# GpSimd forms the rests of the output weights in both feed-forwards, and the first feed-forward's gate and up products are laid side by side

## The chip, the cores and the metric

The kernel runs on one core of a Trainium2 chip. The metric is the device time of one execution in microseconds (us). The kernel before took 1524.12 us, the median of 3 runs (1520.59 to 1524.94).

## The reference, cut to what matters

Two transformer blocks follow one another on 256 tokens of width 1024, in float32. The first has attention, a short convolution and a mixture of 32 experts. The second wraps two attentions between two feed-forwards, and those two are what the change touches:

```python
def swiglu(h, w_in, w_out):
    gu = h @ w_in                      # 1024 x (2 * 2816)
    g, u = jnp.split(gu, 2, axis=-1)
    return (jax.nn.silu(g) * u) @ w_out   # 2816 x 1024

ada = c_act @ w_ada[l] + b_ada[l]      # 1024 x 9216, one row
h = modulate(rmsnorm(x, ffn1_norm[l]), sh1, sc1)
x = x + FFN_RES_WEIGHT * g1[:, None, :] * swiglu(h, ffn1_w_in[l], ffn1_w_out[l])
...                                    # two attentions
h = modulate(rmsnorm(x, ffn2_norm[l]), sh3, sc3)
x = x + FFN_RES_WEIGHT * g3[:, None, :] * swiglu(h, ffn2_w_in[l], ffn2_w_out[l])
```

## The kernel before, in words

The five engines run their own instruction lists side by side and meet only at semaphores. Activations lie transposed: the 1024 channels in 8 chunks of 128 partitions, the 256 tokens along the free axis.

**Hi and lo parts.** Each float32 operand of the feed-forwards is split in two: a rounded part ("hi", type fp32r, written by a ScalarE copy) and a rest ("lo", the original less the rounded part). A product is the sum of three: hi weights by hi inputs, lo weights by hi inputs, hi weights by lo inputs. The inputs' parts lie beside each other in `ff_x_parts` (per chunk, 256 columns of hi, then 256 of lo).

**Steps.** The inner width 2816 is cut into 22 steps of 128, s = 1 to 22, for each of the feed-forwards "ffn1" and "ffn2". `past(key)` adds 22 to the semaphore counts of ffn2. Step s has on TensorE a `gate_up` (gate and up, 8 chunks each, three passes) and a `down` (8 output chunks, three passes over the hi and lo parts of weights and activations). TensorE runs `gate_up(s + 1)` between `gate_up(s)` and `down(s)`. Steps 3 to 22 lie in a loop of 5 iterations with four steps written out (j = 0 to 3); `down(22)` is `down_by_bank`, after the loop. The gate and up sums of a step take two PSUM banks, 4 and 5 or 6 and 7 by the step's parity.

**ffn1 against ffn2.** They differ in `gate_up`. In ffn1 it is 48 matmuls of 256 columns (L1680, L1690, L1698), all summed into the first half of the banks. In ffn2, from the second step on, the hi weights meet hi and lo inputs in one matmul of 512 columns (L1685, 16 of them), which leaves the product with the lo inputs in the second half of the bank; then come the 16 matmuls with the lo weights (L1690). ScalarE copies the second halves out to `ff_b` (L1045), VectorE adds both halves into `gate_up_sum` (`sum_halves`, L2410), and ScalarE applies Silu there (L1049). In ffn1 Silu reads the bank itself (L1040) and VectorE takes "up" from the bank.

**VectorE's list** per step: the rest of the output weights (`ff_out_rest`, L2376, 128x1024, both inputs in SBUF), `sum_halves` (ffn2 only), silu(gate) times up (`act`, L2418), the rest of the next step's input weights (`ff_rest`, L2369, 128x2048), and the rest of the activation (`act_rest`, L2423).

**The ada columns.** ffn1 carries other work along: 10 pieces of `c_act @ w_ada` of 512 columns each, two in an iteration. VectorE sums a piece over 8 chunks in 8 dependent instructions (`mod_steps`, L2434 for the first, L2437 for the other seven) into `mod_acc`; of the 16 instructions of an iteration 5 stand at the end of VectorE's step j=0, 5 at the end of j=1 and 6 at the end of j=2. TensorE folds each piece over the partitions (`ada_columns`, L1740) after the `gate_up` of its j=1 (first piece) and of its j=2 (second), and waits there for the last instruction of the piece:

```python
pe.wait_ge(sem("mod_acc_step"), it * 16 + 8 * (u + 2))
pe.wait_ge(sem("ff_act"), s)
```

TensorE's j=1 `gate_up` is that of step 4it+4, its j=2 one that of 4it+5; VectorE's j counts from s = 4it+2. VectorE's `take_columns` (L2445) adds the bias to the folded piece, in j=2 and j=3.

**Queues.** ScalarE's list per step: round half of a new input weight chunk (`ff_round`, L1026), silu, round a new half of the output weights (`ff_round_out`, L1032; the half of step s comes behind the silu of step s-1), round the activation (L1054). SP issues all weight loads of this stage. GpSimd has nothing from the convolution (L762 to L766) until the first feed-forward's end, then a few small masks (L772 to L786), and one DMA in the second feed-forward (L789). Nothing is planned at run time; the order of each list is written out by hand.

Of the kernel before, what the change touches and what calls it, by code (L numbers as in the profile page):

```python
# [14 lines left out]
T = 256  # L15
# [137 lines left out]
def mixed_blocks_kernel(nc, ins, out):  # L153
# [3 lines left out]
    with ExitStack() as ctx:  # L157
# [577 lines left out]
        def _(pool):  # L735
# [31 lines left out]

            pool.wait_ge(sem("bias_stored"), 16)
# [14 lines left out]
            for at in (64, P + 192):  # L783
                late = ca_bias[64:P, :, at:at + 64]
                step(nc.gpsimd.tensor_scalar(late, late, NEG, 1.0, ALU.add, ALU.mult))
            nc.gpsimd.memset(pool_done[:, :], 0.0).then_inc(sem("masked"), 1)  # L786
            pool.wait_ge(sem("ff_x_lo"), 2 * KD)
            g_at = ROWS_B["final_norm"]
            pool.dma_start(gain_rows, ins["vectors_b"][g_at:g_at + KD, :].rearrange("r c -> (r c)").partition_broadcast(P))\  # L789
                .then_inc(sem("gain_rows_loaded"), 16)  # L790

# [5 lines left out]
        def _(act):  # L797
# [237 lines left out]
            def feed_forward(key):  # L1035
                def silu(s, parity, more=True):

                    act.wait_ge(sem("ff_gate_up_done"), s + past(key))
                    if key == "ffn1":
                        nc.scalar.activation(gate_up_sum[:, parity, 0, :], bank[4 + 2 * parity][:, 0:T], ACT.Silu)\  # L1040
                          .then_inc(sem("ff_silu"), 1)
                        return
                    if more:
                        act.wait_ge(sem("ff_summed"), s - 1)
                    nc.scalar.activation(ff_b[:, :, :], psum[:, 4 + 2 * parity:6 + 2 * parity, T:2 * T], ACT.Copy)\  # L1045
                      .then_inc(sem("ff_b_taken"), 1)
                    act.wait_ge(sem("ff_summed"), s)
                    gate = gate_up_sum[:, parity, 0, :]
                    nc.scalar.activation(gate, gate, ACT.Silu).then_inc(sem("ff_silu"), 1)  # L1049

                def round_act(s, parity):

                    act.wait_ge(sem("ff_act"), s + past(key))
                    nc.scalar.activation(ff_act_hi[:, parity, :], gate_up_sum[:, parity, 1, :], ACT.Copy)\  # L1054
                      .then_inc(sem("ff_act_hi"), 1)

                ff_round_out(key, 3, 0, 16)
                silu(1, 0, more=False)
                round_act(1, 0)
                ff_round_out(key, 3, 1, 16)  # L1060
                with act.Fori(0, FF_LOOPS) as it:
                    for j in range(4):
                        slot = 2 * (j // 2)
                        ff_round(key, slot, j % 2, it * 32 + 32 * (1 + j // 2))
                        silu(it * 4 + j + 2, (j + 1) % 2)
                        ff_round_out(key, slot + 1, j % 2, it * 16 + 16 * (1 + j // 2))
                        round_act(it * 4 + j + 2, (j + 1) % 2)
                silu(4 * FF_LOOPS + 2, 1)
                round_act(4 * FF_LOOPS + 2, 1)

# [112 lines left out]
        def _(pe):  # L1183
# [479 lines left out]
            def feed_forward(key, ada_items):  # L1663
                all_emptied(JOBS[done_jobs[0] - 1])

                def gate_up(s, slot, half, parity, taken, first=False):
# [4 lines left out]
                    if taken is not None and key == "ffn1":  # L1671
                        pe.wait_ge(sem("ff_act"), taken)
                    elif taken is not None:
                        pe.wait_ge(sem("ff_summed"), taken)
                    if first or key == "ffn1":
# [12 lines left out]
                    for g in range(2):  # L1688
                        for k in range(KD):
                            last = pe.matmul(to[g][:, 0:T], lhsT=w_lo[:, k, g, :], rhs=ff_x_hi[:, k, :], start=False,  # L1690
                                             stop=(k == KD - 1 and key == "ffn2"), skip_group_check=True)
                    if first or key == "ffn1":
                        at = 0 if key == "ffn1" else T
                        for g in range(2):
                            for k in range(KD):
                                if g == 0 and first:
                                    pe.wait_ge(sem("ff_x_lo"), k + 1 + past(key, KD))
                                last = pe.matmul(to[g][:, at:at + T], lhsT=w_hi[:, k, g, :], rhs=ff_x_lo[:, k, :], start=False,  # L1698
                                                 stop=(k == KD - 1), skip_group_check=True)
# [201 lines left out]
        def _(dve):  # L1901
# [470 lines left out]
            def ff_out_rest(key, s, slot, half):  # L2372

                dve.wait_ge(sem("ff_out_hi"), s + past(key))
                part = slice(half * D, (half + 1) * D)
                nc.vector.tensor_tensor(ff_out_lo[slot][:, part], ring(slot)[:, part], ff_out_hi[slot][:, part], ALU.subtract)\  # L2376
                  .then_inc(sem("ff_out_lo"), 1)

# [25 lines left out]
            def feed_forward(key, with_ada, gate_at):  # L2404
                def sum_halves(s, parity):

                    if key == "ffn1":
                        return
                    dve.wait_ge(sem("ff_b_taken"), s)
# [3 lines left out]
                def act(s, parity):  # L2413
# [3 lines left out]
                    by = bank[5 + 2 * parity][:, 0:T] if key == "ffn1" else up  # L2417
                    nc.vector.tensor_tensor(up, gate_up_sum[:, parity, 0, :], by, ALU.mult).then_inc(sem("ff_act"), 1)  # L2418
# [29 lines left out]
                ff_out_rest(key, 1, 3, 0)  # L2448
# [6 lines left out]
                with dve.Fori(0, FF_LOOPS) as it:  # L2455
                    for j in range(4):
                        s, parity = it * 4 + j + 2, (j + 1) % 2
                        ff_out_rest(key, s, (3, 1, 1, 3)[j], (j + 1) % 2)
# [8 lines left out]
                ff_out_rest(key, 4 * FF_LOOPS + 2, 3, 1)  # L2467
# [242 lines left out]
```

## Time and profile before

| what | us |
|---|---|
| median of 3 runs | 1524.12 (1520.59 to 1524.94) |
| the profiled execution | 1516.13 |
| its span, first to last instruction | 1514.1 |
| TensorE busy in it | 1459.4 (96%) |
| VectorE busy | 617.6 (41%) |
| ScalarE busy | 443.2 (29%) |
| GpSimd busy | 27.3 (2%) |
| ffn1, first to last matmul of gate, up and down | 903.3 to 1102.8 |
| ffn2, the same | 1317.2 to 1504.2 |

The profiled execution took 2.0 us more than its span, and it is 8.0 us shorter than the median of the runs. An engine's share of busy time is a mean over stages with different limits. Times in the rows below are counted from the span's start.

### The profile page before, as it was taken

The page shows a single profiled execution, that of the slowest core. Times are in us where ns is not written, and L with a number is a line of the kernel's source. Part 1 is how long each engine was busy: PE and PEld are TensorE (multiplying, and loading weights), DVE is VectorE, ACT ScalarE, POOL GpSimd, SP SyncE. Part 2 cuts the span into 40 slices and gives each one's busy share as a digit, 9 for nine tenths or more (in the row PEclk, how much of TensorE's full clock was granted, in tenths as well). Part 3 has the DMA queues.
Part 4 walks back from the last instruction along what each step waited for, and adds up shares of the span by engine and source line. Part 5 has one row for each costly group of instructions (what it writes and reads, how often), then busy time and mean ns, then how long its engine had stood idle before and what let it go on. Part 6 is the DMA issues. An engine that isn't in the chain of part 4 may idle for free.

```text
span 1514.1 us, 23559 instructions
## 1 busy us (share of the span) xinstructions
PE 1459.4 (96%) x9994; PEld 1029.7 (68%) x9994; DVE 617.6 (41%) x1024; ACT 443.2 (29%) x674; POOL 27.3 (2%) x36
## 2 busy tenths in 40 slices
PE   6999999999999999999999999999999998999997
PEld 3986854444444444444434459999999777999997
DVE  5686240011110001101100038777777577565555
ACT  3434031111011111111011134333354364454443
POOL 0011000000000000000000000000020000000000
PEclk9999999999999999999999989999999999999999
DMA  9959799999999999999999997888667731355651
GB/s 357 354 189 351 286 385 431 425 429 431 425 431 427 431 424 430 427 429 430 429 429 427 427 340 245 283 286 295 230 220 276 258 112 53 120 171 181 207 172 56
DMA packets 117427, 481.01 MB, mean 318 GB/s; under 512 B 12108, under 2 KB 59465, under 8 KB 96769
## 3 DMA queue, kind: packets, MB, share of 16 engines
q1 hardware_dynamic: 115936, 476.46, 80.4%
q0 software_dynamic: 736, 2.31, 0.5%
q10 hardware_dynamic: 705, 1.51, 0.3%
q8 instruction: 39, 0.64, 0.2%
q14 instruction: 11, 0.09, 0.0%
HBM read 479.20 MB, written 1.06 MB: 317 GB/s over the span
## 4 chain that ended last, share of the span: by engine, by line
PE 73%; DMA 21%; DVE 3%; ACT 2%; issue 1%; SPq 0%; DVEq 0%; ACTq 0%
DMA arena<-in_w_up_dram 18%; PE psum L1576 14%; PE psum L1712 8%; PE psum L1790 7%; PE psum L1598 6%; PE psum L1690 6%; PE psum L1685 5%; PE psum L1215 3%; PE psum L1680 3%; PE psum L1698 3%; PE psum L1339 3%; PE psum L1557 2%; PE psum L1539 2%; DMA arena<-in_w_mod_dram 2%; DMA arena<-in_ffn_w_in_dram 1%
## 5 line engine op out<-in xcount | busy, mean ns | idle before, releaser
L1576 PE MATMUL psum<-arena,squares 128*64 128x384 f32 x2048 | 339.3, 489 | 21.0 <-DMA arena<-in_w_up_dram 12.3
L1576 PEld LDWEIGHTS psum<-arena,squares 128*64 128x64 f32 x2048 | 146.3, 137 | 216.3 <-issue 186.0
L2303 DVE TENSOR_TENSOR mixT<-mixT,psum 128x384 f32<-128x384 f32 x32 | 26.5, 827 | 496.7 <-PE psum L1576 496.7
L1598 PE MATMUL psum<-arena,small 128*64 128x512 f32 x768 | 171.9, 596 | 0.0
L1598 PEld LDWEIGHTS psum<-arena,small 128*64 128x64 f32 x768 | 52.3, 137 | 96.2 <-issue 94.4
L2369 DVE TENSOR_TENSOR ff_w_lo<-arena,ff_w_hi 128x2048 fp32r<-128x2048 f32 x44 | 100.6, 2285 | 0.0
L1690 PE MATMUL psum<-ff_x_parts,ff_w_lo 128*128 128x256 f32 x704 | 91.5, 283 | 0.0
L1690 PEld LDWEIGHTS psum<-ff_x_parts,ff_w_lo 128*128 128x128 f32 x704 | 88.9, 192 | 1.6
L1026 ACT ACTIVATE ff_w_hi<-arena 128x2048 fp32r<-128x2048 f32 x44 | 84.0, 1908 | 0.2 <-DMA arena<-in_ffn_w_in_dram 0.2
L1685 PE MATMUL psum<-ff_x_parts,ff_w_hi 128*128 128x512 f32 x336 | 79.7, 389 | 0.0
L998 ACT ACTIVATE small<-psum 128x384 f32<-128x384 f32 x32 | 15.8, 493 | 212.5 <-PE psum L1584 212.5
L1790 PE MATMUL psum<-ff_x_parts,mid_w_hi 128*128 128x256 f32 (+1 forms) x576 | 75.9, 287 | 0.1
L1557 PE MATMUL psum<-small 64*128 64x256 f32 x528 | 74.6, 402 | 0.7 <-ACT small L1003 0.7
L1790 PEld LDWEIGHTS psum<-ff_x_parts,mid_w_hi 128*128 128x128 f32 (+1 forms) x576 | 71.1, 190 | 2.9 <-ACT ff_x_parts L880 1.4
L1003 ACT ACTIVATE small<-psum 128x512 f32<-128x512 f32 x32 | 19.1, 598 | 176.6 <-PE psum L1598 176.6
L1685 PEld LDWEIGHTS psum<-ff_x_parts,ff_w_hi 128*128 128x128 f32 x336 | 61.7, 188 | 11.6
L1079 ACT ACTIVATE mid_w_hi<-arena 128x2048 fp32r<-128x2048 f32 (+2 forms) x28 | 45.8, 1644 | 73.1 <-PE psum L1790 56.4
L1557 PEld LDWEIGHTS psum<-small 64*128 64x128 f32 x528 | 45.5, 186 | 29.0 <-issue 24.5
L1539 PE MATMUL psum<-mixT,h_rows 128*128 128x128 f32 x512 | 59.8, 275 | 0.0
L2383 DVE TENSOR_TENSOR mid_w_lo<-arena,mid_w_hi 128x2048 fp32r<-128x2048 f32 (+2 forms) x28 | 54.7, 1955 | 12.4 <-ACT mid_w_hi L1079 12.3
L1539 PEld LDWEIGHTS psum<-mixT,h_rows 128*128 128x128 f32 x512 | 58.5, 192 | 0.1
L996 ACT ACTIVATE mixT<-psum 128x384 f32<-128x384 f32 x32 | 15.7, 491 | 140.4 <-PE psum L1576 140.4
(344 smaller groups left out, 1966.9 us busy)
## 6 DMA issues: line engine op xcount, KB each, us to landing
arena<-in_w_gate_dram SPq DMA_DIRECT2D x32, 3072.0 KB, 32.8
arena<-in_w_up_dram SPq DMA_DIRECT2D x31, 3072.0 KB, 33.9
arena<-in_w_down_dram SPq DMA_DIRECT2D x31, 3072.0 KB, 32.2
arena<-in_ffn_w_in_dram SPq DMA_DIRECT2D x44, 1024.0 KB, 7.6
arena<-in_w_ada_dram SPq DMA_DIRECT2D x18, 2048.0 KB, 12.6
arena<-in_w_mod_dram SPq DMA_DIRECT2D x11, 2048.0 KB, 14.0
arena<-in_ffn_w_out_dram SPq DMA_DIRECT2D x22, 1024.0 KB, 4.9
arena<-in_w_in_dram SPq DMA_DIRECT2D x10, 2048.0 KB, 9.8
```

The costliest lines, as they stand in the source:

```text
L1026: nc.scalar.activation(ff_half(ff_w_hi[slot], half), ff_half(ring(slot), half), ACT.Copy)\
L1079: nc.scalar.activation(hi, raw, ACT.Copy).then_inc(sem("mid_hi"), 1)
L1539: last = pe.matmul(b[:, k * P:(k + 1) * P], lhsT=h_rows[:, tb, (4 * part + k) * P:(4 * part + k + 1) * P], rhs=pick[:, tb, :], start=(tb = ...
L1557: last = pe.matmul(bank[m // 2][:, (m % 2) * T:(m % 2 + 1) * T], lhsT=y_e[64 * half:64 * half + 64, c * P:(c + 1) * P], rhs=pick_wT[64 * h ...
L1576: last = pe.matmul(b[64 * half:64 * half + 64, 0:HALF_E], lhsT=xeT[:, k, u * SLOTS:(u + 1) * SLOTS], rhs=w[:, k, half * HALF_E:(half + 1) ...
L1598: last = pe.matmul(bank[6][64 * half:64 * half + 64, :], lhsT=hiddenT[:, f % 3, 64 * (f // 3):64 * (f // 3) + 64], rhs=down[:, f, half * 5 ...
L1685: last = pe.matmul(to[g][:, :], lhsT=w_hi[:, k, g, :], rhs=ff_x_parts[:, k, :, :], start=(k == 0), stop=False, skip_group_check=True)
L1690: last = pe.matmul(to[g][:, 0:T], lhsT=w_lo[:, k, g, :], rhs=ff_x_hi[:, k, :], start=False, stop=(k == KD - 1 and key == "ffn2"), skip_gro ...
L1712: last = pe.matmul(bank[m // 2][:, (m % 2) * T:(m % 2 + 1) * T], lhsT=w[slot][:, half * D + m * P:half * D + (m + 1) * P], rhs=x[:, parity ...
L1790: last = pe.matmul(b[0:n, c * T:(c + 1) * T], lhsT=w[:, k, lo:lo + n], rhs=x[:, k, :], start=opens and c == 0 and k == 0, stop=closes and ...
L2369: nc.vector.tensor_tensor(ff_half(ff_w_lo[slot], half), ff_half(ring(slot), half), ff_half(ff_w_hi[slot], half), ALU.subtract).then_inc(se ...
L2383: nc.vector.tensor_tensor(lo, raw, hi, ALU.subtract).then_inc(sem("mid_lo"), 1)
```

## The change

In four places: `ff_out_rest` goes from VectorE's list to GpSimd's, for both feed-forwards; `silu` and `sum_halves` take the way with `ff_b` in both; `gate_up` uses the 512-column matmuls in ffn1 too, from its second step on; and the waits that used `ff_act` or bare counts in ffn1 now use `ff_summed` with `past(key)`. The ada columns stay where they are.

```diff
 @block.gpsimd
+            def ff_out_rest(key, s, slot, half):
+                pool.wait_ge(sem("ff_out_hi"), s + past(key))
+                part = slice(half * D, (half + 1) * D)
+                nc.gpsimd.tensor_tensor(ff_out_lo[slot][:, part], ring(slot)[:, part], ff_out_hi[slot][:, part], ALU.subtract)\
+                  .then_inc(sem("ff_out_lo"), 1)
+            def feed_forward(key):
+                for it in range(FF_LOOPS):
+                    for j in range(4):
+                        ff_out_rest(key, it * 4 + j + 2, (3, 1, 1, 3)[j], (j + 1) % 2)
+                ff_out_rest(key, 4 * FF_LOOPS + 2, 3, 1)
+            ff_out_rest("ffn1", 1, 3, 0)
+            feed_forward("ffn1")
             pool.wait_ge(sem("bias_stored"), 16)
             pool.wait_ge(sem("ffn1_sum_done"), 4)
...
             nc.gpsimd.memset(pool_done[:, :], 0.0).then_inc(sem("masked"), 1)
+            ff_out_rest("ffn2", 1, 3, 0)
             pool.wait_ge(sem("ff_x_lo"), 2 * KD)
...
+            feed_forward("ffn2")
 @block.scalar, silu
-                    if key == "ffn1":
-                        nc.scalar.activation(gate_up_sum[:, parity, 0, :], bank[4 + 2 * parity][:, 0:T], ACT.Silu)\
-                          .then_inc(sem("ff_silu"), 1)
-                        return
                     if more:
-                        act.wait_ge(sem("ff_summed"), s - 1)
+                        act.wait_ge(sem("ff_summed"), s - 1 + past(key))
 @block.tensor, gate_up
-                    if taken is not None and key == "ffn1":
-                        pe.wait_ge(sem("ff_act"), taken)
-                    elif taken is not None:
-                        pe.wait_ge(sem("ff_summed"), taken)
-                    if first or key == "ffn1":
+                    if taken is not None:
+                        pe.wait_ge(sem("ff_summed"), taken + past(key))
+                    if first:
...
-                    if first or key == "ffn1":
-                        at = 0 if key == "ffn1" else T
+                    if first:
 @block.vector
-            def ff_out_rest(key, s, slot, half):
...
 feed_forward, sum_halves
-                    if key == "ffn1":
-                        return
-                    dve.wait_ge(sem("ff_b_taken"), s)
+                    dve.wait_ge(sem("ff_b_taken"), s + past(key))
 act
-                    by = bank[5 + 2 * parity][:, 0:T] if key == "ffn1" else up
-                    nc.vector.tensor_tensor(up, gate_up_sum[:, parity, 0, :], by, ALU.mult).then_inc(sem("ff_act"), 1)
+                    nc.vector.tensor_tensor(up, gate_up_sum[:, parity, 0, :], up, ALU.mult).then_inc(sem("ff_act"), 1)
```

## Rows read from the trace of the kernel before

**Rows 1.** Busy time by stretch, inside ffn1: window, length, engines, PEclk, DMA share, GB/s.
```profile
960.00:1000.00 40.00, 40.00 (x339) 40.00 (x338) 30.60 (x37) 16.48 (x20) 0.00 (x0) 1.00 0.87 299
```
**Rows 2.** Timeline of ffn1: start, length, engine, line, operation, shapes, count [idle before].
```profile
952.64 1.11 PE L1712 MATMUL psum<-ff_act_hi,ff_out_hi 128*128 128x256 f32 x8
...
961.23 1.11 PE L1712 MATMUL psum<-ff_act_hi,ff_out_hi 128*128 128x256 f32 x8
...
969.82 0.95 PE L1740 MATMUL psum<-consts,mod_acc 128*128 128x1 f32 x8
...
973.88 4.69 DVE L2437 SCALAR_TENSOR_TENSOR mod_acc<-arena,cond,mod_acc 128x512 f32<-128x512 f32 x6
...
979.29 0.94 PE L1740 MATMUL psum<-consts,mod_acc 128*128 128x1 f32 x8
```
**Rows 3.** VectorE by line, 920 to 1080: count | busy us, mean ns | idle before.
```profile
L2437 DVE SCALAR_TENSOR_TENSOR mod_acc<-arena,cond,mod_acc 128x512 f32<-128x512 f32 x64 | 48.1, 751 | 2.0
...
L2434 DVE TENSOR_SCALAR mod_acc<-arena,cond 128x512 f32<-128x512 f32 x10 | 4.8, 482 | 1.1 <-DMA arena<-in_w_ada_dram 1.1
```
**Rows 4.** Timeline of one step of ffn2.
```profile
1372.45 1.11 PE L1712 MATMUL psum<-ff_act_hi,ff_out_hi 128*128 128x256 f32 x8
...
1373.28 0.69 DVE L2410 TENSOR_TENSOR small<-psum,ff_b 128x512 f32<-128x512 f32 x1 [3.04 <-ACT ff_b L1045]
...
1374.33 1.05 ACT L1032 ACTIVATE ff_out_hi<-arena 128x1024 fp32r<-128x1024 f32 x1
...
1374.46 0.42 DVE L2418 TENSOR_TENSOR small<-small 128x256 f32<-128x256 f32 x1 [0.48 <-ACT small L1049]
1374.80 2.29 DVE L2369 TENSOR_TENSOR ff_w_lo<-arena,ff_w_hi 128x2048 fp32r<-128x2048 f32 x1
...
1375.29 3.79 PE L1685 MATMUL psum<-ff_x_parts,ff_w_hi 128*128 128x512 f32 x16
...
1377.00 0.42 DVE L2423 TENSOR_TENSOR ff_act_lo<-small,ff_act_hi 128x256 fp32r<-128x256 f32 x1
1377.34 1.22 DVE L2376 TENSOR_TENSOR ff_out_lo<-arena,ff_out_hi 128x1024 fp32r<-128x1024 f32 x1
...
1380.84 1.11 PE L1712 MATMUL psum<-ff_act_hi,ff_out_hi 128*128 128x256 f32 x8
```
**Rows 5.** Timelines of GpSimd and VectorE beside each other, in the convolution.
```profile
110.95 2.36 POOL L765 TENSOR_TENSOR arena<-arena,mixT 128x1024 f32<-128x1024 f32 x1
...
115.56 2.61 POOL L765 TENSOR_TENSOR arena<-arena,mixT 128x1024 f32<-128x1024 f32 x1
...
115.46 0.49 DVE L2135 TENSOR_SCALAR small<-small,stats 128x512 f32<-128x512 f32 x1
...
115.86 2.60 DVE L2135 TENSOR_SCALAR small<-small,stats 128x512 f32<-128x512 f32 x1
```
**Rows 6.** The same two engines behind ffn1.
```profile
1110.64 0.70 POOL L780 TENSOR_SCALAR arena<-arena,consts 2x512 f32<-2x512 f32 x1
1111.43 0.75 POOL L781 TENSOR_SCALAR arena<-arena,consts 2x512 f32<-2x512 f32 x1
...
1110.95 0.65 DVE L2389 SCALAR_TENSOR_TENSOR ff_x_parts<-hT,ada,ff_x_parts 128x256 fp32r<-128x256 f32 x1
...
1111.53 0.92 DVE L2389 SCALAR_TENSOR_TENSOR ff_x_parts<-hT,ada,ff_x_parts 128x256 fp32r<-128x256 f32 x1
...
1109.00 0.86 DVE L1975 SCALAR_TENSOR_TENSOR hT<-xT,gains,psum 128x256 f32<-128x256 f32 x2
```
**Rows 7.** Timeline, VectorE at the start of ffn1.
```profile
912.76 3.25 DVE L1981 SCALAR_TENSOR_TENSOR xT<-xT,cols_a,rstd 128x256 f32<-128x256 f32 x8
```
**Rows 8.** TensorE's pauses in the expert stage: waits (total, times, longest), timeline, stretch.
```profile
PE psum L1576 <- DMA arena<-in_w_up_dram: 12.3, 7, 1.9
...
544.16 12.23 PE L1576 MATMUL psum<-arena,squares 128*64 128x384 f32 x64 [3.38 <-issue]
...
545.00:550.00 5.00, 5.00 (x24) 1.99 (x20) 0.00 (x0) 0.00 (x0) 0.00 (x0) 0.66 1.04 436
```

More of the change, by code:

```diff
@@ L1038, in silu @@
                     act.wait_ge(sem("ff_gate_up_done"), s + past(key))
-                    if key == "ffn1":
-                        nc.scalar.activation(gate_up_sum[:, parity, 0, :], bank[4 + 2 * parity][:, 0:T], ACT.Silu)\
-                          .then_inc(sem("ff_silu"), 1)
-                        return
                     if more:
-                        act.wait_ge(sem("ff_summed"), s - 1)
+                        act.wait_ge(sem("ff_summed"), s - 1 + past(key))
                     nc.scalar.activation(ff_b[:, :, :], psum[:, 4 + 2 * parity:6 + 2 * parity, T:2 * T], ACT.Copy)\
                       .then_inc(sem("ff_b_taken"), 1)
-                    act.wait_ge(sem("ff_summed"), s)
+                    act.wait_ge(sem("ff_summed"), s + past(key))
                     gate = gate_up_sum[:, parity, 0, :]
@@ L1690, in gate_up @@
                             last = pe.matmul(to[g][:, 0:T], lhsT=w_lo[:, k, g, :], rhs=ff_x_hi[:, k, :], start=False,
-                                             stop=(k == KD - 1 and key == "ffn2"), skip_group_check=True)
-                    if first or key == "ffn1":
-                        at = 0 if key == "ffn1" else T
+                                             stop=(k == KD - 1), skip_group_check=True)
+                    if first:
                         for g in range(2):
                             for k in range(KD):
-                                if g == 0 and first:
+                                if g == 0:
                                     pe.wait_ge(sem("ff_x_lo"), k + 1 + past(key, KD))
-                                last = pe.matmul(to[g][:, at:at + T], lhsT=w_hi[:, k, g, :], rhs=ff_x_lo[:, k, :], start=False,
+                                last = pe.matmul(to[g][:, T:2 * T], lhsT=w_hi[:, k, g, :], rhs=ff_x_lo[:, k, :], start=False,
                                                  stop=(k == KD - 1), skip_group_check=True)
@@ L2370, in ff_rest @@
                                         ALU.subtract).then_inc(sem("ff_w_lo"), 1)
-            def ff_out_rest(key, s, slot, half):
[L2374 to L2377, printed above, removed]
             def rest_w(name):
@@ L2446, in take_columns @@
                                             ALU.add).then_inc(sem("ada_col_read"), 1)
-                ff_out_rest(key, 1, 3, 0)
                 sum_halves(1, 0)
@@ L2466, in feed_forward @@
                             mod_steps(it, 5 * j, 5 * j + 5 + j // 2)
-                ff_out_rest(key, 4 * FF_LOOPS + 2, 3, 1)
                 sum_halves(4 * FF_LOOPS + 2, 1)
```

1 line of the change is left out of this document (removed).

## The prediction

> **What bounds the kernel now.** I read the busy times by stretch first. In 40 us of ffn1 TensorE is busy for all 40.00 at full clock, VectorE for 30.60, GpSimd for none [rows 1]. So ffn1 is bound by TensorE, and VectorE, at three quarters, is the engine to watch. The timeline gives TensorE's pace as the distance between two downs: 961.23 - 952.64 = 8.59 us for a plain step. With ada columns in it a step takes 979.29 - 969.82 = 9.47 us [rows 2]. An iteration of the loop is 2 x 8.59 + 2 x 9.47 = 36.12 us. The same timeline shows where VectorE comes close: the six `mod_steps` of j=2 start at 973.88 and end at 978.57, and TensorE takes their result at 979.29 [rows 2]. That slack of 0.72 us is the smallest in the loop. In ffn2 a step takes 1380.84 - 1372.45 = 8.39 us [rows 4].
>
> **The change, part by part.** Sums are against the profiled execution (1516.13 us). It ran 8.0 us under the median of the runs; I carry the difference over to the median.
>
> *Fewer, wider matmuls.* ffn2 already has the form that ffn1 gets, and its plain step is 8.59 - 8.39 = 0.20 us shorter [rows 2, 4]. Steps 2 to 22 get it: 21 x 0.20 = 4.2 us, if nothing else binds. A step with ada columns would take 9.27.
>
> *A longer chain behind a gate_up.* From the end of `gate_up` (G = 1372.45, where the down starts) rows 4 give VectorE's times: sum at G+0.83, `act` at G+2.01, `ff_rest` at G+2.35, `act_rest` at G+4.55, next operation at G+4.89. ScalarE ends the new rounded output half at G+2.93. The sum adds 0.69 us of work to VectorE in ffn1, the move takes off 1.22 [rows 4]; by work alone VectorE has 0.5 us less per step.
>
> *GpSimd's subtraction.* 44 of 128x1024. Its own tensor_tensor of that size took 2.36 and 2.61 us [rows 5], against VectorE's 1.22 [rows 4]. GpSimd is idle here [rows 1], and the rest of step s may be ready as late as down(s), a whole step after its rounded half, so its length alone costs nothing. But the two engines hold each other up. In rows 5 a VectorE tensor_scalar started at 115.46 took 0.49; GpSimd's subtraction-sized operation, issued at 115.56, took 0.25 longer than the other one and ended at 118.17; and the next VectorE operation, the same as the first, took 2.60, to 118.46. Taken apart: GpSimd ended 2.22 after VectorE's first (115.95), was served before an instruction already queued, and VectorE resumed 0.20 before GpSimd's end (118.46 - 0.49 = 117.97). Is it so for operations with two SBUF inputs, such as those of ffn1? Rows 6 say yes: two of L2389 beside two short GpSimd operations took 0.65 and 0.92, while eight of that size with two SBUF inputs took 3.25 without GpSimd, 0.41 each [rows 7]; the second GpSimd operation took 0.05 more than the first. An operation with one input in PSUM (L1975, 0.86 for two) ran on undisturbed [rows 6]. So `sum_halves` is free of it; `act`, `ff_rest`, `act_rest` and the `mod_steps` are not.
>
> By the Trainium skill (SBUF — State Buffer, Who interferes with whom) a VectorE instruction with two SBUF inputs and a GpSimd instruction that reads SBUF exclude each other for the whole instruction. By that rule the sum is the one below; rows 5 and 6 agree, with blocks of 2.1 us and 0.2 to 0.5 us.
>
> *What it does to a step.* GpSimd may start at G+2.93, but `ff_rest` has run since G+2.35 and ends at G+4.64. GpSimd then ends at 4.64 + 2.22 = 6.86, and `act_rest` starts at 6.66 in place of 4.55: 2.11 us lost. In ffn2 VectorE would still be done at G+7.1, before the next sum at 8.39 + 0.83 = 9.22, and the third pass of the down that needs `act_rest` comes later still. So ffn2 keeps its time: 0. The ends of this cost are 0 and 0.5 us for its start; I take 0. The DMA of the gains, now queued on GpSimd behind the first rest, is used only at the end.
>
> *What it does to ffn1.* The `mod_steps` stand behind it. They take 0.75 each with 0.48 for the first of a piece [rows 3]: 3.5 us at j=0, 3.5 at j=1, 4.69 to the end of the six at j=2 [rows 2]. A VectorE step is now 1.18 (sum to act) + 0.34 + 2.20 + 2.11 + 0.34 = 6.17 us before its mod steps. From j=0 on, 6.17 + 3.5 = 9.7 is more than the 8.39 of TensorE, so VectorE falls behind and the chain runs through it. With G of j=0 at 0:
> - j=0's sum starts at 0.83; the three steps take 3 x 6.17 + 3.5 + 3.5 + 4.69 = 30.2, so the second piece is ready at 31.0.
> - TensorE waits for the first piece until 0.83 + 2 x 6.17 + 3.5 + 2.25 = 18.9, where it came at 2 x 8.39 = 16.8: a stall of 2.1 us. It is back at 18.9 + 9.27 = 28.2, and waits 2.8 us for the second.
> - From there ada columns, down and gate_up take 9.27; the next G of j=0 is at 40.3. VectorE has no mod steps at j=3 and has caught up by then.
>
> Per iteration 40.3 - 36.1 = 4.2 us more, and 5 x 4.2 = 21.0. The saving of the wide matmuls is inside that.
>
> *Start and end.* VectorE runs eight operations with two SBUF inputs (3.25 us) behind step 1 [rows 7], and GpSimd's second rest falls into them. They end 2.1 us later, sum(2) with them, at about 2.2 us past the 0.83 that the chain above starts from: 2.2 more, once. Step 2's own saving is 0.2. At the end of ffn1 the down of step 21 covers 2.84 us (1375.29 - 1372.45), while `act` starts at 2.01 [rows 4] and has itself and ScalarE's rounding, 0.4 each, before `down_by_bank`: 0.2 more than before. Together 21.0 + 2.2 - 0.2 + 0.2 = 23.2.
>
> *The clock.* The stalls of 2.1 and 2.8 us are new. Pauses up to 1.9 us in the expert stage (7 of them) go with full clock; after one of 3.38 us the granted clock was 0.66 over 5 us [rows 8], part of that at the lower level (1.2 GHz), which costs 0.34 x 5 = 1.7 us. 2.8 lies between. A loss behind the first piece is swallowed by the wait for the second; behind the second it counts, five times: 0 to 8.5. I take the middle, 4.3, since the nearest rows on both sides are about equally far.
>
> *Other queues.* SP loads the next ada chunk when the first piece is summed, 2 us later than now; what is queued behind it waits for a down that is later anyway. ScalarE's silu waits for `sum_halves` and so is late with VectorE, and with it the next rounding of input weights; these are wanted a down and more later. 0.
>
> Sum: 23.2 + 4.3 = 27.5. The profiled execution would be 1543.6, the median 1524.12 + 27.5 = 1551.6 us.
>
> **The rivals.**
>
> *GpSimd does not hold VectorE up in ffn1* (not slower). For it: rows 5 are of a one-input operation, and rows 6 of short ones; neither is two tensor_tensors. Against it: rows 6 show the same order of service. Then j=2's mod steps end at G + 4.89 + 4.69 = 9.58 against TensorE's 9.27, a wait of 0.3 to 0.4 us, where 0.8 is saved in an iteration: 5 x 0.43 = 2.2 faster, with start and end still 2.2: 1521.9. It decides from the point at which VectorE loses under about 0.5 us a step.
>
> *GpSimd holds VectorE up by part.* In rows 6 VectorE lost (0.65 - 0.47) + (0.92 - 0.47), 0.63 us, beside 1.45 us of GpSimd's work: 0.43 for one. (0.47 is one such operation from issue to end, 0.41 the pace.) At that rate, or if GpSimd is let in only in VectorE's gaps, a subtraction costs 1.0: the step is 5.06, the second piece is ready at 0.83 + 15.2 + 11.7 = 27.7, the iteration is 37.0, 5 x 0.9 = 4.5 more, 1.0 at the start; TensorE's stall is 1.6 and the clock stays. 1529.6.
>
> *The full block without the clock's part* is 1547.3; *with all of it*, 1555.8; these are the ends of the likeliest case, with 4 us around them for the lengths of the blocks.
>
> **How the numbers follow.** Full block 0.76 (1543 to 1560); block by part 0.10; no block 0.10; anything else, such as TensorE's wide matmuls not saving their 0.2, 0.04. The range, 1529 to 1563, takes in the partial block and leaves out the last two. A difference under 0.3% (4.6 us) can't be told from none. The no-block case, at 2.2 us, is inside that: faster 0.04, same 0.11, slower 0.85.
>
> **What would show it.** In the changed kernel's profile: L1685's form in ffn1 with 227 ns or so from one to the next; GpSimd busy for some 100 us more, with operations of 2.4 to 4 us from issue to end; VectorE's `act_rest` or the operation behind `ff_rest` about 2.1 us longer in ffn1 and ffn2, `sum_halves` still 0.69; TensorE's idle time before L1740, released by VectorE's L2437, of about 2 us and 2.8 us in each iteration; ffn2 as long as before; PEclk under 1.00 in some stretches of ffn1. I am wrong if `act_rest` keeps its 0.42 and there is no wait before L1740.

## The result, and the profile after

The changed kernel took 1548.0 us, the median of 4 runs (1545.6 to 1554.2), against 1522.4 (1519.6 to 1524.9) for the kernel before on the same chip: 1.0183 times as long [1.0159, 1.0206]. That is 25.6 us more by the medians and 28 by the ratio. 1551.6 was forecast, 27.5 more. The profiled execution took 1545.67 us, with a span of 1543.5.

The page of the changed kernel: the span; busy time by engine; the granted clock; two of the costliest groups (instruction and line, shapes, count | busy us, mean ns of one | idle before it).

```profile
span 1543.5 us, 22902 instructions
...
PE 1467.5 (95%) x9648; PEld 1022.5 (66%) x9658; DVE 670.9 (43%) x1002; ACT 455.4 (30%) x696; POOL 193.8 (13%) x80
...
PEclk9999999999999999999999999999999999899999
...
L772 POOL TENSOR_TENSOR ff_out_lo<-arena,ff_out_hi 128x1024 fp32r<-128x1024 f32 x44 | 166.7, 3790 | 1212.9 <-ACT ff_out_hi L1051 1212.9
...
L2425 DVE TENSOR_TENSOR ff_act_lo<-small,ff_act_hi 128x256 fp32r<-128x256 f32 x44 | 106.5, 2420 | 1.9 <-ACT ff_act_hi L1069 1.9
```

VectorE gave 44 subtractions of 1.22 us away (53.7 us) and took 22 sums of 0.69 (15.1 us), and yet is busy for 53.3 us more than the 617.6 before. `act_rest` (L2425), which took 0.42 us before [rows 4], takes 2.42 in the mean over its 44: 2.62 in 40 of them, and 0.42 or so in the four that have no `ff_rest` before them. A digit of PEclk stands for 39 us, and its 9 for anything from 0.9 up: too coarse to show what the clock did in ffn1. Shorter stretches show it, in experiment 7.

TensorE's waits in ffn1, between 900 and 1130 us: what waited for what, total us, times, longest us. In the kernel before VectorE's last mod step was 0.72 us ahead [rows 2].

```profile
PE psum L1752 <- DVE mod_acc L2439: 18.5, 10, 2.6
PE psum L1703 <- DVE ff_w_lo L2381: 1.4, 2, 1.2
```

The ada columns wait all ten times. The timeline of the second iteration, some of its lines on TensorE, VectorE and GpSimd, with the idle time before a line and its releaser in brackets, answers to [rows 2]:

```profile
960.21 1.11 PE L1724 MATMUL psum<-ff_act_hi,ff_out_hi 128*128 128x256 f32 x8
...
961.12 0.69 DVE L2413 TENSOR_TENSOR small<-psum,ff_b 128x512 f32<-128x512 f32 x1 [5.42 <-ACT ff_b L1060]
...
962.64 2.28 DVE L2381 TENSOR_TENSOR ff_w_lo<-arena,ff_w_hi 128x2048 fp32r<-128x2048 f32 x1
...
963.29 3.88 POOL L772 TENSOR_TENSOR ff_out_lo<-arena,ff_out_hi 128x1024 fp32r<-128x1024 f32 x1 [7.87 <-ACT ff_out_hi L1051]
964.84 2.62 DVE L2425 TENSOR_TENSOR ff_act_lo<-small,ff_act_hi 128x256 fp32r<-128x256 f32 x1
967.38 0.47 DVE L2436 TENSOR_SCALAR mod_acc<-arena,cond 128x512 f32<-128x512 f32 x1
...
970.92 0.68 DVE L2413 TENSOR_TENSOR small<-psum,ff_b 128x512 f32<-128x512 f32 x1
...
979.55 1.05 PE L1752 MATMUL psum<-consts,mod_acc 128*128 128x1 f32 x8 [2.41 <-DVE mod_acc L2439]
...
986.85 4.68 DVE L2439 SCALAR_TENSOR_TENSOR mod_acc<-arena,cond,mod_acc 128x512 f32<-128x512 f32 x6
...
991.59 1.05 PE L1752 MATMUL psum<-consts,mod_acc 128*128 128x1 f32 x8 [2.48 <-DVE mod_acc L2439]
...
992.50 2.02 PE L1724 MATMUL psum<-ff_act_hi,ff_out_hi 128*128 128x256 f32 x8
...
1002.52 0.76 PE L1724 MATMUL psum<-ff_act_hi,ff_out_hi 128*128 128x256 f32 x5
```

The lines to see are the fourth and fifth. GpSimd is released at 963.29, while `ff_rest` runs on VectorE until 964.92. It ends at 967.17, 2.25 us behind that; `act_rest`, issued next on VectorE, lasts until 967.46, 2.62 us where 0.42 would do: 2.20 late. The mod steps come behind it, and then the next `sum_halves`, which has no idle time before it any more: VectorE sets the pace.

**Where the time went.** I count iterations from down to down: the first starts with the down behind `gate_up(2)`, which runs while VectorE does its j=0 (in what follows, a "down of j=0"). It starts at 915.78, and the one behind the fifth iteration at 1124.81: 209.03 us, against 5 x 36.12 = 180.60 before: 28.4 us more. The iterations last 44.43, 42.31, 40.77, 40.76 and 40.76. That is 40.77 for the chain, 5 x 4.65 = 23.2 in all; a later start of 2.1; and 1.55 in each of the first two, in which the clock had fallen behind the second wait. Outside the loop the two profiled executions differ by 1.0 us in all: 0.7 less before it and 1.7 more behind it.

ffn2, the timeline of one of its steps; it answers to [rows 4]:

```profile
1385.12 1.11 PE L1724 MATMUL psum<-ff_act_hi,ff_out_hi 128*128 128x256 f32 x8
...
1387.47 2.29 DVE L2381 TENSOR_TENSOR ff_w_lo<-arena,ff_w_hi 128x2048 fp32r<-128x2048 f32 x1
...
1388.12 3.88 POOL L772 TENSOR_TENSOR ff_out_lo<-arena,ff_out_hi 128x1024 fp32r<-128x1024 f32 x1 [4.50 <-ACT ff_out_hi L1051]
1389.67 2.62 DVE L2425 TENSOR_TENSOR ff_act_lo<-small,ff_act_hi 128x256 fp32r<-128x256 f32 x1
...
1393.50 0.76 PE L1724 MATMUL psum<-ff_act_hi,ff_out_hi 128*128 128x256 f32 x5
```

The same hold-up of 2.20 us, and a step of 8.38, as before: nothing waits for VectorE here. From the first down of ffn2 to its last bank it is 172.97 us in both kernels (1330.52 to 1503.49 before, 1359.96 to 1532.93 now).

### The profile page after: what moved, and what is told of

Same layout as the page of the kernel before. It is cut to its first block, busy times and chain, and to the rows that moved or that the text cites. A ratio compares the mean times of both kernels' runs of the same rounds, so it can differ in the third digit from the quotient of the medians.

```text
span 1543.5 us, 22902 instructions
## 1 busy us (share of the span) xinstructions
PE 1467.5 (95%) x9648; PEld 1022.5 (66%) x9658; DVE 670.9 (43%) x1002; ACT 455.4 (30%) x696; POOL 193.8 (13%) x80
## 4 chain that ended last, share of the span: by engine, by line
PE 62%; DMA 20%; DVE 11%; issue 3%; ACT 3%; SPq 0%; DVEq 0%; ACTq 0%
DMA arena<-in_w_up_dram 17%; PE psum L1591 14%; PE psum L1802 7%; PE psum L1698 6%; PE psum L1613 6%; PE psum L1724 5%; PE psum L1703 3%; PE psum L1230 3%; DVE mod_acc L2439 3%; PE psum L1354 3%; DVE ff_act_lo L2425 3%; PE psum L1572 2%; PE psum L1554 2%; DMA arena<-in_w_in_dram 2%; DMA arena<-in_ffn_w_in_dram 1%
## 5 line engine op out<-in xcount | busy, mean ns | idle before, releaser
L772 POOL TENSOR_TENSOR ff_out_lo<-arena,ff_out_hi 128x1024 fp32r<-128x1024 f32 x44 | 166.7, 3790 | 1212.9 <-ACT ff_out_hi L1051 1212.9
L1698 PE MATMUL psum<-ff_x_parts,ff_w_hi 128*128 128x512 f32 x672 | 159.9, 390 | 0.0
L1698 PEld LDWEIGHTS psum<-ff_x_parts,ff_w_hi 128*128 128x128 f32 x672 | 123.7, 188 | 23.4
L2425 DVE TENSOR_TENSOR ff_act_lo<-small,ff_act_hi 128x256 fp32r<-128x256 f32 x44 | 106.5, 2420 | 1.9 <-ACT ff_act_hi L1069 1.9
L1060 ACT ACTIVATE ff_b<-psum 128x512 f32<-128x512 f32 x44 | 26.4, 599 | 161.3 <-PE psum L1703 159.6
```

Of the source, the lines that this page charges most:

```text
L772: nc.gpsimd.tensor_tensor(ff_out_lo[slot][:, part], ring(slot)[:, part], ff_out_hi[slot][:, part], ALU.subtract)\
L1698: last = pe.matmul(to[g][:, :], lhsT=w_hi[:, k, g, :], rhs=ff_x_parts[:, k, :, :], start=(k == 0), stop=False, skip_group_check=True)
L2425: nc.vector.tensor_tensor(ff_act_lo[:, parity, :], gate_up_sum[:, parity, 1, :], ff_act_hi[:, parity, :], ALU.subtract).then_inc(sem("ff_a ...
```

## The experiments

Ratios are to the kernel before, run on the same chip, whose medians were 1521.5 to 1522.0 us. Profiled executions of nearly equal programs differ by up to 8 us in when ffn1 starts (its first down of j=0 at 915.8 to 924.2). They differ so before anything in which the kernels do: the sums of squares for ffn1's norm start on TensorE at 891.8 in the kernel before and at 900.0 in experiment 1; so within ffn1 I compare lengths of iterations, from a down to the down four steps later, and not spans.

**1. Rests back on VectorE.** The changed kernel without its GpSimd part: what do the wide matmuls and the sum cost alone?

```diff
 @block.gpsimd
-            ff_out_rest("ffn1", 1, 3, 0)
-            feed_forward("ffn1")
...
-            ff_out_rest("ffn2", 1, 3, 0)
...
-            feed_forward("ffn2")
 @block.vector, where it stands in the kernel before
+                nc.vector.tensor_tensor(ff_out_lo[slot][:, part], ring(slot)[:, part], ff_out_hi[slot][:, part], ALU.subtract)
```

> The changed kernel with both feed-forwards' output-weight rests back on VectorE; ffn1 keeps the 512-column matmuls and the summing of halves. Theory (GpSimd blocks VectorE, VectorE's mod steps hold TensorE up): no operation behind ff_rest is stretched, so act_rest is 0.42 us again. Per iteration VectorE's sum is late by 0.3 and 0.6 us at j=1 and j=2, the second piece is 1.0 us late, and the iteration takes 36.3 us against 36.1 before and 40.8 to 44.4 in the changed kernel: 1 us over the kernel before in all, the whole 25 us of the change gone. Rival (the longer chain of copy, sum and Silu in ffn1 costs the time, GpSimd little): 15 us or more stay. Rival (the wide matmuls do not save): iterations of 37 us and more, some 5 us over the kernel before.

Measured: 1526.3 us, 1.0026 [1.0011, 1.0042], 4 us over before by the ratio (4.8 by the medians), and some 22 under the changed kernel. TensorE's waits in its ffn1:

```profile
PE psum L1748 <- DVE mod_acc L2442: 5.0, 6, 1.4
```

Its timeline, TensorE in the first iteration and a later one:

```profile
953.07 2.05 PE L1720 MATMUL psum<-ff_act_hi,ff_out_hi 128*128 128x256 f32 x8
963.05 1.11 PE L1720 MATMUL psum<-ff_act_hi,ff_out_hi 128*128 128x256 f32 x8
...
1026.50 1.05 PE L1748 MATMUL psum<-consts,mod_acc 128*128 128x1 f32 x8 [0.83 <-DVE mod_acc L2442]
...
1035.89 1.11 PE L1720 MATMUL psum<-ff_act_hi,ff_out_hi 128*128 128x256 f32 x8
```

The steady iteration is 36.42 us (999.47 to 1035.89), 0.30 more than before. The first is 39.03 (from 924.02), 2.61 longer: a wait of 1.42 before the second piece, and behind it a step of 9.98 where the steady ones take 8.47, with a granted clock of 0.66 from 953 to 958. 5 x 0.30 + 2.61 = 4.1. I had expected 1 us and had left the clock out.

**2. The move alone.** The kernel before, with the GpSimd part of the change: narrow matmuls, no sum in ffn1.

```diff
-                ff_out_rest(...)      # in VectorE's list
+            feed_forward("ffn1")      # in GpSimd's, with ff_out_rest as in the change
```

> The kernel before with only the move: both feed-forwards' rests on GpSimd, ffn1 with its narrow matmuls and no summing of halves. Theory: act_rest grows to 2.6 us here too. VectorE's step before its mod steps is 0.34 + 2.20 + 2.2 + 0.34 = 5.1 us, against 6.2 in the changed kernel, where the wait for copy and sum is added; from G+0.62 three steps and 11.7 us of mod steps give the second piece at 27.5 where TensorE comes at 26.7: an iteration of 37.1 us, 5 us over five iterations and 1 at the start, 6 us over the kernel before. So the two parts do not add up: 6 here, 1 for the other part alone, 25 together. Rival (GpSimd's block costs the same wherever it is): 20 us or more over the kernel before. Rival (no cost without the summing): within 1 us of the kernel before.

Measured: 1536.7 us, 1.0088 [1.0059, 1.0118], 13 us over before, about twice what I expected. TensorE's waits in its ffn1, then GpSimd and VectorE at one step j=3:

```profile
PE psum L1759 <- DVE mod_acc L2449: 6.9, 5, 1.4
```
```profile
1031.22 2.38 POOL L772 TENSOR_TENSOR ff_out_lo<-arena,ff_out_hi 128x1024 fp32r<-128x1024 f32 x1 [5.00 <-ACT ff_out_hi L1051]
...
1032.78 2.96 DVE L2388 TENSOR_TENSOR ff_w_lo<-arena,ff_w_hi 128x2048 fp32r<-128x2048 f32 x1
```

The steady iteration is 37.77 us (1002.97, 1040.74, 1078.52, 1116.28), 1.65 over before: 5 x 1.65 = 8.3. I had expected 37.1; the sum had left out that VectorE stands still for 0.47 us before `take_columns` in j=2. The first iteration is 3.2 longer than the steady ones: 1.5 of it is the clock (955.00 to 965.20, 10.20 us, against 8.67), and 1.65 lie in its first step, with a wait of 1.4 for `ff_w_lo`. In j=3 the order is the other way round: GpSimd comes first, and `ff_rest` is held up for 0.68 us (2.96 in place of 2.28) while `act_rest` keeps its 0.41. The same happened in that first step, where `ff_rest` took 4.16. So the engine that is already at work goes on, and the other waits.

The parts do not add up. The loop of ffn1 is 4.1 us longer with the one, 11.4 with the other and 28.4 with both; a steady iteration +0.30, +1.65 and +4.65. The slack of 0.72 us [rows 2], which each alone may use, is only a small part of that. The rest is how many hold-ups are paid for. In the move alone VectorE's j=0 with its mod steps lasts 8.63 us (1003.59 to 1012.22), close to TensorE's 8.59, so that only the second piece is waited for, five times in all. In the changed kernel it lasts 9.80 (961.12 to 970.92) against 8.39: VectorE falls behind in every step, and both pieces are waited for.

**3. GpSimd in ffn2 only.** The changed kernel, with `ff_out_rest` on VectorE where the key is "ffn1" and on GpSimd where it is "ffn2".

```diff
 @block.gpsimd
-            ff_out_rest("ffn1", 1, 3, 0)
-            feed_forward("ffn1")
 @block.vector
+                if key == "ffn1":
+                    ff_out_rest(key, ...)
```

> The changed kernel with ffn1's rests on VectorE and only ffn2's on GpSimd. Theory: in ffn2 there are no mod steps, VectorE is done at G+7.2 with the block in it and the next sum comes at G+9.2; act_rest takes 2.6 us in ffn2 and 0.42 in ffn1, ffn2's step stays 8.39, and the time is that of e1_vector_rests (4 us over the kernel before) within 2. Rival (GpSimd's work in ffn2 costs too): 8 us or more over the kernel before.

Measured: 1531.3 us, 1.0049 [1.0030, 1.0069]. That is 3.5 us over experiment 1 by the ratios and 5.0 by the medians, with intervals that overlap, where I expected less than 2. VectorE between 1360 and 1500 us, by line:

```profile
L2430 DVE TENSOR_TENSOR ff_act_lo<-small,ff_act_hi 128x256 fp32r<-128x256 f32 x17 | 44.5, 2618 | 0.0
```

And its timeline, two of TensorE's downs in ffn2:

```profile
1388.70 1.11 PE L1722 MATMUL psum<-ff_act_hi,ff_out_hi 128*128 128x256 f32 x8
1397.09 1.11 PE L1722 MATMUL psum<-ff_act_hi,ff_out_hi 128*128 128x256 f32 x8
```

VectorE is held up (in experiment 1 the same instruction takes 0.42 there) and the step is 8.39 us with and without it (1388.16 to 1396.55 in experiment 1). From the first down of ffn2 to its last bank both take 172.97 us (1346.77 to 1519.74 here, 1346.23 to 1519.20 there). The loop of ffn1 is 3.2 us longer than experiment 1's (187.91 against 184.71), though both are the same program there: two more steps at a low clock (1025.04 to 1035.06, 1063.02 to 1073.05: 10.02 us each against 8.47). The two profiled executions as wholes differ by 0.7 us. So ffn2's part costs nothing that shows; that the difference between the medians comes from the clock in ffn1 is likely, but not shown.

**4. GpSimd only writes.** In place of the subtraction GpSimd sets the rest to zero, which reads nothing; the rests of the output weights are left out.

```diff
-                nc.gpsimd.tensor_tensor(ff_out_lo[slot][:, part], ring(slot)[:, part], ff_out_hi[slot][:, part], ALU.subtract)\
+                nc.gpsimd.memset(ff_out_lo[slot][:, part].bitcast(F32), 0.0)\
```

> The changed kernel with GpSimd's subtraction replaced by a memset of the same 128x1024: the rest of the output weights is left out. It writes SBUF and reads nothing, and should take 0.9 us. Theory (VectorE and GpSimd exclude each other where both read SBUF): act_rest 0.42 us, VectorE never delayed by GpSimd, a wait of 0.4 us before the second piece's ada columns, 2 us under the kernel before to 2 over it (the clock may fall after the small waits). Rival (any GpSimd operation on these tiles holds VectorE up): act_rest 0.42 + 0.7 us and more, as in the run with one input.

Measured: 1520.7 us, 0.9995 [0.9976, 1.0014]. GpSimd and VectorE in its ffn1, by line:

```profile
L772 POOL MEMSET ff_out_lo<- 128x1024 f32 x16 | 15.3, 956 | 127.8 <-ACT ff_out_hi L1051 127.8
...
L2425 DVE TENSOR_TENSOR ff_act_lo<-small,ff_act_hi 128x256 fp32r<-128x256 f32 x16 | 6.7, 418 | 0.0
```

TensorE's waits there:

```profile
PE psum L1752 <- DVE mod_acc L2439: 1.0, 5, 0.2
```

`act_rest` is back at 0.42 us. The memset runs beside `ff_rest`, which keeps its 2.29 us (1031.05 to 1032.01 beside 1030.42 to 1032.71), where the subtraction ended 2.25 behind it. The iteration is 35.78 in the mean of five, with one wait of 0.19 in it. This is the first rival's case built: for it I had worked out 36.12 - 0.43 = 35.69, a wait of 0.3 to 0.4 and 2.2 us under before; the ratio says 0.8 under, between 3.7 under and 2.1 over.

**5. GpSimd reads one input.** Between the two: a one-input operation of the same size; the rests hold zeros and so are left out again.

```diff
+                nc.gpsimd.tensor_scalar(ff_out_lo[slot][:, part], ring(slot)[:, part], 0.0, 0.0, ALU.mult, ALU.add)\
```

> The changed kernel with GpSimd's subtraction replaced by a tensor_scalar of the raw weights, 128x1024, one SBUF input: the rest is left out (zeros take its place). About 1.1 us of its own, close to the memset. Theory: it reads SBUF, so it waits for ff_rest to end and act_rest is 0.8 to 0.9 us late (1.3 us from issue to end); VectorE's step is 4.9 us before its mod steps, the second piece is 0.9 to 1.3 us late at TensorE, and the time is 2 to 8 us over the kernel before, between the memset and the changed kernel. Rival (only two-input operations of GpSimd block): act_rest 0.42 and the time of the memset.

Measured: 1531.9 us, 1.0058 [1.0036, 1.0081], 9 us over before. The same two lines:

```profile
L772 POOL TENSOR_SCALAR ff_out_lo<-arena 128x1024 fp32r<-128x1024 f32 x15 | 39.0, 2601 | 102.7 <-ACT ff_out_hi L1051 102.7
...
L2425 DVE TENSOR_TENSOR ff_act_lo<-small,ff_act_hi 128x256 fp32r<-128x256 f32 x15 | 19.0, 1265 | 0.0
```

TensorE's waits:

```profile
PE psum L1752 <- DVE mod_acc L2439: 6.0, 6, 1.1
```

`act_rest` is 1.27 - 0.42 = 0.85 us late, and the iteration is 36.70 at full clock, in the second and the fifth. In the other three the clock fell for a step (38.97, 38.24 and 38.27 us). So of the 8.3 us that its loop is longer than before, the five iterations make 5 x 0.58 = 2.9, the clock some 4.6 and the start 0.8. Experiments 4, 5 and the changed kernel make a scale in which only GpSimd's operation differs: VectorE held up by 0, 0.85 and 2.20 us a step, iterations of 35.78, 36.70 and 40.77. With 0.85 a step of VectorE and its mod steps last 6.17 - 2.11 + 0.85 + 3.5 = 8.41 us, as long as TensorE's 8.39: the first two steps keep up, and one 0.85 is paid for, at the second piece (0.92 an iteration). From there every step adds up: 1.35 more costs 4.07, about three times 1.35.

By the Trainium skill (SBUF — State Buffer, Who interferes with whom) a VectorE instruction with two inputs in SBUF is kept out by a GpSimd instruction that reads SBUF, not by one that only writes. The three runs agree: 0 us beside the memset, 0.85 and 2.20 beside the readers.

**6. Short mod steps.** The changed kernel, GpSimd's subtraction in place, with each mod step on 64 columns of 512; seven eighths of the ada products are left out.

```diff
-                          mod_acc[:, u, :]  ...  w[:, j, :]
+                          mod_acc[:, u, 0:64]  ...  w[:, j, 0:64]
```

> The changed kernel with its rests on GpSimd; the mod steps of ffn1 work on 64 of the 512 columns, so 7 in 8 of the ada columns' products are left out. Theory: the block is as before (act_rest 2.6 us), but 16 mod steps take 3 us and not 11.5, VectorE's step with them is under 8.39 us, TensorE waits for nothing and an iteration takes 35.3 us: 4 us under the kernel before in ffn1, at most 1 lost at its start. Rival (TensorE, ScalarE or the DMAs are slowed by GpSimd's work directly): 10 us or more over the kernel before.

Measured: 1522.1 us, 0.9990 [0.9970, 1.0010], where I expected some 3 us fewer; the interval reaches to 4.6 fewer. GpSimd and VectorE by line:

```profile
L772 POOL TENSOR_TENSOR ff_out_lo<-arena,ff_out_hi 128x1024 fp32r<-128x1024 f32 x16 | 62.2, 3888 | 79.1 <-ACT ff_out_hi L1051 79.1
L2425 DVE TENSOR_TENSOR ff_act_lo<-small,ff_act_hi 128x256 fp32r<-128x256 f32 x16 | 41.9, 2621 | 0.0
```

Its timeline, TensorE's downs of j=0:

```profile
995.72 1.11 PE L1724 MATMUL psum<-ff_act_hi,ff_out_hi 128*128 128x256 f32 x8
...
1031.04 1.11 PE L1724 MATMUL psum<-ff_act_hi,ff_out_hi 128*128 128x256 f32 x8
...
1066.36 1.11 PE L1724 MATMUL psum<-ff_act_hi,ff_out_hi 128*128 128x256 f32 x8
```

`act_rest` is still 2.20 us late and now costs nothing: the iteration is 35.32 us, as long as in experiment 9 without the hold-up, 0.80 under before. Only the first is longer, by 1.30, from the late start. The loop is 2.7 us shorter than before (177.90 against 180.60), which the medians don't show. The hold-up alone is harmless; it costs because the mod steps stand behind it and a wait of TensorE behind them.

**7. Filling the waits.** The changed kernel, with matmuls of zeros before each wait for the mod steps, so that TensorE doesn't pause.

```diff
+                    pe.wait_ge(sem("ff_act"), s)
+                    keep_busy(9, 4 + 2 * u)
                     pe.wait_ge(sem("mod_acc_step"), it * 16 + 8 * (u + 2))
-                    pe.wait_ge(sem("ff_act"), s)
```

> The changed kernel, with matmuls of zeros (9, 4 + 2u of about 0.24 us, some 2 us) put before each wait of TensorE for VectorE's mod steps, so that the wait holds no long pause. They take the time of the wait and nothing else, unless a wait was shorter than they are. My theory: of the 25.6 us over the kernel before, some 3 are lost to the clock that fell behind the wait for the second piece of the ada columns (two of five iterations, 1.55 us each), the rest is the chain on VectorE. Then the granted clock is 1.00 behind those waits, iterations 2 to 5 last 40.8 us each, and the time is about 3 us below the changed kernel: 1.016 of the kernel before. Rival A, the clock costs nothing of the total, since the chain sets the pace: 1.018. Rival B, the clock is the main cost and the iterations return towards 37 us: below 1.008.

Measured: 1544.7 us, 1.0159 [1.0121, 1.0197]. The medians put it 3 us below the changed kernel, and the interval holds both 1.016 and 1.018; the traces decide. A stretch of ffn1: window, length, busy us (instructions) of TensorE, its weight loads, VectorE, ScalarE and GpSimd, granted clock, DMA share, GB/s. With the zeros:

```profile
960.00:1000.00 40.00, 39.03 (x254) 33.77 (x253) 34.44 (x34) 16.26 (x20) 15.81 (x4) 1.00 0.75 262
```

The same stretch of the changed kernel:

```profile
960.00:1000.00 40.00, 35.12 (x226) 32.28 (x225) 34.42 (x34) 16.31 (x20) 15.81 (x4) 0.96 0.72 246
```

With the zeros the clock is 1.00, in the three stretches of 40 us that follow too, and the iterations last 42.88, 40.77, 40.77, 40.76 and 40.77: 205.95 us, 3.08 less than the changed kernel's 209.03. So the clock's part is 3.1 us, and the other 25.3 of the loop's 28.4 are VectorE's chain with its late start.

**8. The second piece a step later.** Can the wait be moved away? The changed kernel, with the second piece folded at TensorE's j=3 in place of j=2, and the 16 mod steps spread 5, 3, 4, 4 over VectorE's four steps in place of 5, 5, 6, 0. `take_columns` for that piece goes to the end of VectorE's j=3, and both pieces are folded in bank 4.

```diff
 @block.tensor, gate_up and down of j=2, then of j=3
-                                ada_columns(it, 1, s - 1)
...
+                                ada_columns(it, 1, s - 1)
 @block.vector
-                            mod_steps(it, 5 * j, 5 * j + 5 + j // 2)
+                            mod_steps(it, (0, 5, 8, 12)[j], (5, 8, 12, 16)[j])
```

> The changed kernel with its rests still on GpSimd, but the second ada piece folded by TensorE after the gate_up of its j=3 and no longer of its j=2, and VectorE's 16 mod steps spread 5, 3, 4, 4 over all four steps. Theory: the block stays (act_rest 2.6 us), but VectorE's idle time at j=3 is used: its iteration is 4 x 6.26 + 11.5 = 36.6 us and it is bound by VectorE's own total, 0.6 us over the kernel before; with the start 3 to 6 us over the kernel before, 20 less than the changed kernel, stalls before the ada columns under 0.5 us. Rival (the time goes by the block itself, wherever the mod steps are waited for): within 5 us of the changed kernel.

Measured: 1553.2 us, 1.0199 [1.0176, 1.0223]; I expected 3 to 6 us over before, and it is 31. TensorE's waits in its ffn1:

```profile
PE psum L1752 <- DVE mod_acc L2439: 14.8, 10, 2.6
```

Its timeline, TensorE in the second iteration and the start of the third:

```profile
980.44 1.05 PE L1752 MATMUL psum<-consts,mod_acc 128*128 128x1 f32 x8 [0.92 <-DVE mod_acc L2439]
981.35 1.39 PE L1724 MATMUL psum<-ff_act_hi,ff_out_hi 128*128 128x256 f32 x8
...
991.36 1.11 PE L1724 MATMUL psum<-ff_act_hi,ff_out_hi 128*128 128x256 f32 x8
...
1001.61 1.05 PE L1752 MATMUL psum<-consts,mod_acc 128*128 128x1 f32 x8 [1.71 <-DVE mod_acc L2439]
1002.52 1.95 PE L1724 MATMUL psum<-ff_act_hi,ff_out_hi 128*128 128x256 f32 x8
```

My error was to add up work over the iteration only. Each piece ends in mod steps that VectorE does in the very step in which TensorE wants them. From the sum at G+0.83 to the end of `act_rest` are 6.26 us, and the four mod steps before the second piece are 3.1 more: ready at G+10.2, wanted at G+8.4. So there is a wait before every piece however light the rest of the iteration is. Besides, nearly every step behind one lasts 10.0 us in place of 8.47 (981.35 to 991.36 and 1002.52 to 1012.52), also behind the wait of 0.92.

**9. Its repair.** The same places for the ada columns, the rests on VectorE, and each rest formed at the end of the step before, behind the mod steps.

```diff
+                        ff_out_rest(key, s + 1, (1, 1, 3, 3)[j], j % 2)   # VectorE, last in its step
```

> The same places of the ada work as in e5_ada_late, with the rests on VectorE (each formed at the end of the step before). A candidate to beat the kernel before. Theory: nothing holds TensorE up in ffn1, iterations of 2 x 8.39 + 2 x 9.27 = 35.3 us, 5 x 0.8 = 4 us under the kernel before, no idle time of TensorE before the ada columns. Rival (the wide matmuls save nothing, or the ada columns still wait): the same as before or above it.

Measured: 1520.4 us, 0.9985 [0.9969, 1.0001]: 28 us faster than the changed kernel, and from the kernel before it can't be told apart. TensorE's waits in its ffn1:

```profile
...
PE psum L1748 <- DVE mod_acc L2442: 0.2, 1, 0.2
```

Its timeline, TensorE at one piece and at two downs four steps apart:

```profile
987.55 0.95 PE L1748 MATMUL psum<-consts,mod_acc 128*128 128x1 f32 x8
...
996.83 1.11 PE L1720 MATMUL psum<-ff_act_hi,ff_out_hi 128*128 128x256 f32 x8
...
1032.15 1.11 PE L1720 MATMUL psum<-ff_act_hi,ff_out_hi 128*128 128x256 f32 x8
```

The iteration is 35.32 us, as in experiment 6: the whole 0.80 of the wide matmuls arrives. Of the 5 x 0.8 = 4.0 us the ratio shows 2.3, and its interval reaches from 4.7 under to 0.2 over.

## Why the prediction was right

The time, 1548.0 against 1551.6, the sign and the mechanism came out as predicted. By its steps:

- *Wide matmuls, 0.20 a step.* Right: without waits the iteration is 35.32 (experiments 6 and 9) against 36.12, 0.80 for four steps. In the changed kernel the step without ada columns is 8.39 too (960.21 to 968.60), but the waits swallow what is saved.
- *GpSimd holds VectorE up by 2.11 us a step.* 2.20 measured, in ffn1 and in ffn2. The order was as read from the convolution [rows 5]: GpSimd ended 2.25 behind VectorE's running instruction (2.22 predicted) and was served before `act_rest`. [rows 5] show it for a VectorE operation with one input, so of the two it is [rows 6] that bear on the rule for two inputs, and the changed kernel bears it out. The rival of no hold-up is refuted by the trace of the changed kernel, and experiment 4 shows what it would have been worth. The rival of a hold-up by part, 1.0 us a step, is refuted too. Experiment 5 is near its size, 0.85; that its 1531.9 us are near the 1529.6 put down for this rival is partly luck: 4.6 of the 8.3 us in its trace are the clock, which the rival had at nothing.
- *ffn2 costs nothing.* Right: 172.97 us before and after, and in experiment 3.
- *The chain in ffn1, 40.3 us an iteration.* 40.77. The waits before the two pieces were 2.41 and 2.48 in the second iteration, for 2.1 and 2.8. The second piece was ready at G+31.0 by the sum and at G+31.4 in the trace (960.21 to 991.59). Of that, three hold-ups of 0.09 more make 0.27, and the first sum at G+0.91 in place of 0.83 another 0.08. From the ada columns to the next down it was 9.39 (40.77 - 31.38), not 9.27, since these columns take 1.05 behind a wait, and 0.95 without. In all 23.2 in place of 21.0.
- *The start, 2.2.* 2.11, the excess of the first iteration with the clock held (experiment 7). The eight operations of [rows 7] took 5.41, 2.16 more. *The end, 0.2*: 3.03 us between the last two downs before `down_by_bank`, against 2.85: 0.18.
- *The clock, 4.3, between 0 and 8.5.* 3.1 (experiment 7). That the middle came close is luck: I took half of 1.7 us in each of five iterations, because 2.8 us lay between pauses of 1.9 and 3.38; what came was 1.55 in two of them and nothing in three, and the clock fell behind a wait of 0.94 us too (before 949.26 in the first iteration; granted clock 0.73 from 949.2 to 954.3). In those three it fell behind the first piece already, and the loss was swallowed there, as the prediction had it: the second wait shrank to 0.98, 0.94 and 0.96.

27.5 was the predicted sum; the terms measured in the trace make 23.2 + 2.1 + 0.2 + 3.1 = 28.6. The chain was put 2.2 too low and the clock 1.2 too high, so the errors cancel in part. The 25.6 between the medians lie 3 below the trace's sum, within what executions of one program differ by; the 28 of the ratio agree with it.

The steps that failed are those of experiments. In 8 the work was added up over an iteration, where a piece is bound within its own step. In 2 I had half of the cost, without VectorE's wait for the folded piece and without the clock. In 1 and 5 the clock was left out.

## What to carry to other kernels

Before work is moved to an idle GpSimd, look at which VectorE instruction will be queued beside it with two inputs in SBUF, and then at what stands behind that one and who waits for it. The hold-up is paid by the waiter at the end of that list, not by the instruction that gets longer: the same 2.20 us cost nothing in ffn2, 1.65 us an iteration in ffn1 with the narrow matmuls (experiment 2), and 4.35 with the wide ones and the sum (36.42 to 40.77). Costs on one chain don't add up: one that stays under the other engine's pace is paid once, and above it in every step (4.1 and 11.4 us alone in ffn1's loop, 28.4 together). So a part tried alone says little for the whole.

## What was not expected of the hardware

- The clock fell behind waits shorter than the 1.9 us that went with full clock in the expert stage [rows 8]. Behind a wait of 0.92 us and the 8 matmuls of one column that follow it the granted clock was 0.66 from 981.3 to 986.3 (experiment 8), which is partly the lower level of 1.2 GHz, and the step took 1.5 us longer; behind 0.82 us and the same 8 matmuls in experiment 1 it stayed at 1.00 (991 to 996). In experiment 3 it fell behind two waits of 0.84 us and not behind two of 0.85 and 0.83, and in experiment 5 behind two of 1.11 and not behind two others of 1.11. What decides between them isn't settled; each fall cost about 1.5 us.
- The profile counts GpSimd's waiting as its work: 3.88 us from issue to end, in ffn1 and ffn2, for an operation that took 2.42 in its first instance (at 909.76, as `ff_rest` was ending), and whose like took 2.36 in the convolution [rows 5]. The 166.7 us of the page are not what these subtractions need; the prediction's "some 100 us more" of GpSimd would be right for their work, and the page shows 166.5 more.
- The one-input operation, 2.60 us from issue to end beside `ff_rest` (experiment 5), held VectorE up for 0.85 us; the memset took 0.96 and held up nothing.
